# The first chunk of an MLP up projection, each 512-token matmul written as two of 256 tokens

## The reference: what is computed

```
u = rmsnorm(h, g_mlp[l])
h = h + square(relu(u @ w_up[l])) @ w_down[l]      # w_up 1024 x 4096, w_down 4096 x 1024
```

## Time and profile before

| | |
|---|---|
| median of 3 runs | 1298.93 us (1298.62 to 1299.15) |
| the profiled execution | 1299.73 us, of which its span is 1297.9 us |
| PE busy | 1253.6 us, 97% of the span, 5675 matmuls |
| PEld busy | 1006.1 us, 78%, 5675 weight loads |
| DVE, ACT, POOL busy | 834.2, 515.7, 89.3 us |
| mean granted clock of TensorE | 0.987 |

### The profile page before, as it was taken

One profiled execution on the slowest core, in us unless ns is written; L12 is line 12 of the kernel. 1 busy time (PEld: TensorE's weight loads), 2 busy tenths in 40 slices (PEclk: granted clock), 3 DMA queues, 4 the chain that ended last, 5 costly groups with the idle time before them and its releaser, 6 DMA issues.

```text
span 1297.9 us, 15337 instructions
## 1 busy us (share of the span) xinstructions
PE 1253.6 (97%) x5675; PEld 1006.1 (78%) x5675; DVE 834.2 (64%) x1385; ACT 515.7 (40%) x848; POOL 89.3 (7%) x125
## 2 busy tenths in 40 slices
PE   5999989999999999999999999899999999999997
PEld 4877667778888888888888766587878888888886
DVE  5568878976845554555656688798675555555554
ACT  5245656654422222222333456666532222222223
POOL 0001212210000000000000012222000000000000
PEclk8999898999999999999999989999999999999999
DMA  5431100122433333333314210002233333333321
GB/s 167 113 81 57 33 1 17 34 81 65 131 97 97 97 97 98 98 98 97 97 54 114 58 53 13 17 17 66 84 88 105 98 97 97 97 98 97 97 82 65
DMA packets 142300, 102.39 MB, mean 79 GB/s; under 512 B 5346, under 2 KB 138516, under 8 KB 142228
## 3 DMA queue, kind: packets, MB, share of 16 engines
q1 hardware_dynamic: 142000, 101.40, 26.4%
q10 hardware_dynamic: 100, 0.03, 0.0%
q0 software_dynamic: 128, 0.00, 0.0%
HBM read 99.32 MB, written 2.10 MB: 78 GB/s over the span
## 4 chain that ended last, share of the span: by engine, by line
PE 59%; issue 28%; DVE 8%; ACT 2%; DMA 1%; POOL 1%; SPq 0%; POOLq 0%; DVEq 0%; ACTq 0%
PE bank L1145 54%; PE bank L1206 2%; PE bank L1227 2%; DVE pt_lo L837 2%; DVE nmx L824 1%; PE bank L1159 1%; ACT pt_hi L550 1%; DMA stage<-in_w_in 1%; DVE w_lo L767 1%; PE bank L1168 1%; PE bank L1321 1%; DVE k_pack L888 1%; DVE e_t L817 0%; DVE diag L788 0%; POOL rs L475 0%
## 5 line engine op out<-in xcount | busy, mean ns | idle before, releaser
L520 ACT ACTIVATE w_hi<-stage 128x1024 fp32r<-128x1024 f32 (+2 forms) x198 | 196.9, 1000 | 493.3 <-PE bank L1145 450.8
L1145 PE MATMUL bank<-u_hi,w_hi 128*128 128x512 f32 x768 | 305.9, 398 | 7.3 <-DVE u_lo L935 5.6
L1145 PE MATMUL bank<-u_hi,w_lo 128*128 128x512 f32 x768 | 300.0, 391 | 0.0
L1145 PE MATMUL bank<-u_lo,w_hi 128*128 128x512 f32 x768 | 299.9, 390 | 0.0
L767 DVE TENSOR_TENSOR w_lo<-stage,w_hi 128x1024 fp32r<-128x1024 f32 (+2 forms) x192 | 225.0, 1177 | 56.7 <-ACT w_hi L520 56.4
L1145 PE MATMUL bank<-hid_hi,w_hi 128*128 128x512 f32 x512 | 199.2, 389 | 0.0
L1145 PE MATMUL bank<-hid_lo,w_hi 128*128 128x512 f32 x512 | 199.2, 389 | 0.0
L1145 PE MATMUL bank<-hid_hi,w_lo 128*128 128x512 f32 x512 | 199.2, 389 | 0.0
L1145 PEld LDWEIGHTS bank<-u_hi,w_hi 128*128 128x128 f32 x768 | 144.7, 188 | 46.2 <-issue 17.5
L1115 DVE TENSOR_TENSOR h<-h,bank 128x512 f32<-128x512 f32 x128 | 87.7, 687 | 136.1 <-PE bank L1145 136.1
L1145 PEld LDWEIGHTS bank<-u_hi,w_lo 128*128 128x128 f32 x768 | 144.7, 188 | 30.9
(11 more groups left out here) (174 smaller groups left out, 1522.9 us busy)
## 6 DMA issues: line engine op xcount, KB each, us to landing
stage<-in_w_up SPq DMA_DIRECT2D x64, 512.0 KB, 4.0
stage<-in_w_down SPq DMA_DIRECT2D x64, 512.0 KB, 3.4
stage<-in_w_in SPq DMA_DIRECT2D x32, 512.0 KB, 3.9
stage<-in_w_out SPq DMA_DIRECT2D x16, 512.0 KB, 3.4
xin<-in_x SPq DMA_DIRECT2D x4, 512.0 KB, 5.7
stage<-in_w_ukv SPq DMA_DIRECT2D x4, 512.0 KB, 3.2
out<-yout SPq DMA_DIRECT2D x4, 512.0 KB, 3.6
stage<-in_w_uq SPq DMA_DIRECT2D x4, 384.0 KB, 3.0
```

The lines of the kernel that those rows point to most:

```text
L520: last = nc.scalar.activation(hi(w_hi, s)[:, :, d:d + n], st(r)[:, :, f:f + n], ACT.Copy)
L1145: mm = nc.tensor.matmul(acc, a, b, start=first and t == 0 and m == 0, stop=last and t == len(terms) - 1 and m == 2)
```

## The change

In chunk 0 of the up projection alone, `up_sum` issues each step's three matmuls twice: for the tokens 0 to 255 into the first half of the bank, then for the tokens 256 to 511 into its second half. The weight tiles are the same for both. The start mark stands on the first matmul of step 0's first half alone, and the stop mark on the last of step 7's second half. The other chunks are as they were. Waits, signals, the bank and the order of the steps are as they were.

```diff
@@ -1410,8 +1410,14 @@
                     for k in part:
                         if c == 0:
                             pe.wait_ge(u_lo_made, val(u_lo_made, l, KD + k + 1))
-                        mm = three(bank[BANK[use]][:, :], [(wtile(SLOT[BLOCK_AT[(f"up{c}", i)]], HALVES[k]), u(HALVES[k]))],
-                                   k == 0, k == KD - 1)
+                        wt = wtile(SLOT[BLOCK_AT[(f"up{c}", i)]], HALVES[k])
+                        if c == 0:
+                            for half in range(2):
+                                q = slice(half * SEQ // 2, (half + 1) * SEQ // 2)
+                                mm = three(bank[BANK[use]][:, q], [(wt, tuple(t[:, q] for t in u(HALVES[k])))],
+                                           k == 0 and half == 0, k == KD - 1 and half == 1)
+                            continue
+                        mm = three(bank[BANK[use]][:, :], [(wt, u(HALVES[k]))], k == 0, k == KD - 1)
                     if part[-1] == KD - 1:
                         mm.then_inc(proj_done, 1)
```

## The result

The changed kernel took 1301.51 us (median of 20 runs, 1299.47 to 1302.18), the one before 1299.24 us in its 20 runs (1298.40 to 1301.02): a ratio of 1.0014, 95% interval 1.0007 to 1.0020. The medians differ by 2.3 us; the ratio makes it 1.8 us (0.9 to 2.6). It is a real loss, and a small one. The profiled execution took 1302.12 us with a span of 1300.3, against 1299.73 and 1297.9 before.

What follows compares the result with a forecast made beforehand. PE was taken to bound the kernel through its 227 ns distance between matmul starts; 0.98 + 0.16 + nothing gave 1.14 us per layer, 2.3 for both, so 1301.2 us from the 1298.93 median, range 1298.6 to 1305.5.

Steps and rivals of the forecast that it cites:

- The number on which all hung: Chunk 0: distance between starts of 256-column matmuls, forecast 120.2 ns, so a pair costs 13.6 ns more than one whole matmul.
- the rule itself: Chunk 0's matmuls: a surcharge of 13.6 ns besides streaming, paid per instruction and not per column.
- rival 1: Chunk 0: surcharge goes with the columns, 113 to 116 ns between starts, 1298.9 to 1299.8 us; chance 0.25.
- The floor: Chunk 0: a weight load does not fit into less than some 111 to 113 ns, so the distance cannot be below.
- The 72 on the path: Chunk 0, tiles 0 to 2: 72 matmuls per layer wholly on the path, 72 x 13.6 = 0.98 us.
- The 12 before the broadcast: Chunk 0, tile 3 before the float32 broadcast: PE is late, so 12 x 13.6 = 0.16 us per layer.
- rival 2: Chunk 0: load and stream get in each other's way, 125 to 133 ns, 1302.8 to 1305.5 us; chance 0.32.
- The 12 after it: Chunk 0, tile 3 after the broadcast: cost nothing, as the 0.8 us wait before up1 covers the 0.16 us.
- Rival 3: Chunk 0: no overlap of load and stream, 218 ns between starts, 19.3 us per layer, 1337.5 us; chance 0.04.
- Rival 4: Layer 1's attention: shifted against the clock grant, 1.4 us per 3 us stretch at the lower clock; faster form's chance 0.04.
- The signs of being wrong: Rest of the kernel moving more than chunk 0, or chunk 0's weight loads becoming longer than 188 ns.
- The rule of the skill: Matmul distance N/2.4 + 2.5 ns at full clock: 2.5 ns more per pair, some 0.4 us in all, 1299.3 us.

Runs made afterwards that it cites:

- the quarters: Chunk 0 alone in four pieces of 128 columns, where the kernel before has whole 512-column matmuls: 1360.38 us in one execution.
- the uneven pieces: Chunk 0 alone split unevenly, against the kernel before: 384 and 128 columns, 1309.34 against 1299.63 us; 320 and 192, 1304.57 against 1300.71 us.

## Why the prediction was right

- **The number on which all hung**, the distance of 256-column matmuls: 120.2 ns forecast, 119.9 measured. It was chosen over 113 because the float32 broadcast asked for less than a surcharge per column would. The right value was in part luck. The profile after gives the same reading anew: from the broadcast at 323.54 to the second short matmul at 324.51 there are 0.97 us for 2 x 426 + 120 = 972 ns, so nothing is left for the long ones where before there were 10 ns each. And the rule itself is only half true: the table above shows the surcharge equal for both widths with 128 loaded columns, and not with 64 or 32.
- **The range**, 1298.6 to 1305.5 us, held no change too, so the time alone would not have told the forecast from rival 1; the 120 ns do.
- **The floor** at 111 to 113 ns, from the train of the statistics: 111.5 in the quarters. It lay below and took no part in the change.
- **The 72 on the path**: 0.98 us per layer forecast, 0.95 measured.
- **The 12 before the broadcast**: 0.16 forecast, 0.09 measured. This term was mis-sized. Whole matmuls have the slower rhythm of 232 ns here (the prediction saw it, and yet put 227 into this term), and the halves do not: from 320.79 to 323.42 they stand 22 steps of 119.5 ns apart. A pair costs 239 against 232, and 12 x 7.5 is 0.09. I had taken this rhythm as a sign for rival 2, that short matmuls would be hurt by it; they are the ones that escape it.
- **The 12 after it**: nothing, as forecast, with 4.44 us from the broadcast to up1 in both profiles.
- **The sum**: 2.3 us forecast; 2.1 in the rows, 2.3 and 1.9 in the two comparisons of medians, 1.8 and 1.4 by their ratios.
- **The rivals.** Rival 1 (as before) falls by the 120 ns. Rival 2 (125 or more) falls too, also in long trains: all chunks in halves cost 13.3 ns per pair. Rival 3 falls. Rival 4 was there, with the other sign and small: 0.8 us more in layer 1's attention in one profile, 0.15 less in the other. It is part of the spread of single executions, which I put at 0.5 us from three runs; 20 runs show 2.6.
- **The signs of being wrong.** One of them came: the weight loads of chunk 0 became longer than 188 ns, 192. It was a poor sign, since the distance is the forecast one all the same; the loads of the statistics, which wait on no stream, were 191 ns long already before.
- **The rule of the skill.** The Trainium skill, "TensorE: Matmul & The Clock Gate", section "Back-to-back issue gap", has a formula that gives an estimate of 109 ns for 256 columns; the trace has 119.9, and the measurement decides. By the formula the change would have cost an estimated 0.4 us; the rows show 2.1.

## What to carry to other kernels

Split a float32r matmul's moving side only for a reason: with 128 loaded columns every matmul paid 13 ns besides its streaming, 6% at 512 columns and 12% at 256, and with 128 columns the weight load of 111 ns set the pace, so that a matmul of 128 columns cost nearly as much as one of 256. Before costing an instruction on PE, read the distance between starts, not durations, and find the two trains in the trace that bound it, one where the stream sets the pace and one where the load does. And look where the engine that seems always busy does stop: 0.84 us per layer before up1 could be had for moving one step of another engine, nearly as much as the change lost.

## What the runs showed of the hardware

- A weight load of 128 columns sets a pace of 111.5 ns at the full clock and of 213 ns at the lower one where the matmuls are short enough (the quarters). It is covered by the one matmul before its own (the uneven pieces).
- TensorE's clock can fall although PE is busy in every record. In the quarters PE was busy 32.11 of 32.11 us with matmuls of 128 columns, 111.5 ns apart; then the clock fell at 337.6 and came back at 358.1, after up1's whole matmuls had begun at 355.3, and layer 1 did the same. In the halves, 120 ns apart, it never fell in chunk 0. The Trainium skill, "TensorE: Matmul & The Clock Gate", section "Part 1: The HAM clock gate (the "warmup" mystery)", says that the clock follows how busy PE has been; these rows show that the busy share of the profile is not that measure. It made the quarters 20 us slower than the distances at the full clock gave.
- A matmul of 512 columns does not always cost the same: 227 ns in a long train, 232 for ten steps after the statistics and again after the stall before up1 (327.70 to 330.01 us in the kernel before, 231 ns), 230 and 232 all along with 64 and 32 loaded columns. Why is open.
